# Moving head 1's query blocks behind the first two rows, and head 1's selection to later dots, in a two-block transformer kernel

## What is computed

```python
def second_block(x, ...):
    xn = rms_norm_2(x, ln_mix_g[l])
    proj = xn @ w_in[l]
    a_out = gmlp_spatial_gating(proj[..., :a0], proj[..., a0:a1], gmlp_norm_g[l], gmlp_w_s[l], gmlp_b_s[l])
    b_out = banded_chunk_attention(proj[..., q0:k0], proj[..., k0:v0], proj[..., v0:], ...)
    x = x + jnp.concatenate([a_out, b_out], axis=-1) @ w_out[l]
    x = x + peer_ffn(rms_norm_2(x, ln_ffn_g[l]), peer_w_query[l], peer_sub_keys[l], peer_u[l], peer_v[l])

def block(xb):                                   # peer_ffn, 128 tokens at a time
    q = (xb @ w_query).reshape(PEER_TOKEN_BLOCK, PEER_HEADS, 2, PEER_HALF)
    sc = jnp.einsum('thpd,hpkd->thpk', q, sub_keys)
    s_top, i_top = lax.top_k(sc, PEER_TOPK)
    cand = s_top[:, :, 0, :, None] + s_top[:, :, 1, None, :]
    cand_idx = i_top[:, :, 0, :, None] * PEER_NKEYS + i_top[:, :, 1, None, :]
    best, pos = lax.top_k(cand, PEER_TOPK)       # of the 256 sums
    eidx = jnp.take_along_axis(cand_idx, pos, axis=-1)
    g = jax.nn.softmax(best, axis=-1)
    u = jnp.take(expert_u, eidx, axis=0)
    h = jax.nn.gelu(jnp.einsum('thkd,td->thk', u, xb))
    vv = jnp.take(expert_v, eidx, axis=0)
    return jnp.einsum('thk,thkd->td', g * h, vv)
```

## Time and profile before

| | us |
|---|---|
| median of 3 runs | 1135.32 (1135.18 to 1135.58) |
| the profiled execution | 1135.66 |
| its span, first to last instruction | 1133.9 |
| PE / DVE / ACT / POOL busy | 1044.0 / 756.1 / 571.2 / 374.1 |
| gathers (queue 0) | 272.95 MB, 58.3% of 16 engines' span |

### The profile page before, as it was taken

The page is one execution under the profiler, slowest core; times in us unless marked ns, Lnnn a source line. Parts: engine busy times, 40 slices in busy tenths (PEclk is TensorE's granted clock), DMA queues, the critical chain, the costliest instruction groups (busy, mean ns, idle before and its releaser), DMA issues.

```text
span 1133.9 us, 13438 instructions
## 1 busy us (share of the span) xinstructions
PE 1044.0 (92%) x3994; PEld 653.8 (58%) x3994; DVE 756.1 (67%) x1612; ACT 571.2 (50%) x1327; POOL 374.1 (33%) x285
## 2 busy tenths in 40 slices
PE   9999999999999999999999999998877878787786
PEld 8788888888888887765455555553322322232222
DVE  5765666665545587567777676677668667776755
ACT  7654564544445478445455535444443443444443
POOL 1000000000000000044355545446566666667642
PEclk9999999999999999999999999999999999999999
DMA  9554357865635667789999999999999999999998
GB/s 346 199 162 149 112 181 232 265 212 179 189 105 170 229 216 285 270 323 413 422 419 422 421 420 421 422 421 421 420 422 423 422 421 422 423 421 422 422 422 350
DMA packets 95788, 368.96 MB, mean 325 GB/s; under 512 B 6688, under 2 KB 30264, under 8 KB 63104
## 3 DMA queue, kind: packets, MB, share of 16 engines
q0 software_dynamic: 38368, 272.95, 58.3%
q1 hardware_dynamic: 57376, 95.45, 25.4%
HBM read 367.30 MB, written 1.06 MB: 325 GB/s over the span
## 4 chain that ended last, share of the span: by engine, by line
PE 55%; DMA 21%; ACT 7%; POOL 6%; issue 6%; DVE 4%; POOLq 0%; SPq 0%; ACTq 0%; DVEq 0%
DMA uv_ring<-in_peer_uv,expert 21%; PE gemm L1755 12%; PE gemm L2245 11%; PE gemm L1757 11%; PE gemm L1756 11%; POOL uv_ring L497 6%; PE gemm L2138 3%; PE gemm L2097 2%; DVE uv_ring L1634 2%; PE trb L1749 1%; ACT L946 1%; ACT L924 1%; ACT diag L951 1%; ACT wgt L949 1%; DVE w_both L992 1%
## 5 line engine op out<-in xcount | busy, mean ns | idle before, releaser
L2245 PE MATMUL gemm<-uv_ring,diag 128*128 128x512 f32 x1020 | 486.0, 613 | 83.1 <-ACT diag L951 80.7
L497 POOL DMA_INDIRECT uv_ring<-in_peer_uv,expert x256 | 359.9, 1406 | 320.4 <-PE gemm L2245 178.1
L2245 PEld LDWEIGHTS gemm<-uv_ring,diag 128*128 128x128 f32 x1020 | 182.4, 192 | 357.6 <-ACT diag L951 191.8
L1634 DVE CUSTOM_DVE_ANT_0 uv_ring<-uv_ring,row_of_tile 128x1024 f32<-128x1024 f32 x208 | 254.6, 1224 | 143.9 <-DMA uv_ring<-in_peer_uv,expert 142.4
L992 DVE TENSOR_TENSOR w_both<-raw,w_both 128x1024 fp32r<-128x1024 f32 (+1 forms) x172 | 180.7, 1063 | 130.8 <-ACT w_both L556 130.0
L556 ACT ACTIVATE w_both<-raw 128x1024 fp32r<-128x1024 f32 (+1 forms) x172 | 158.2, 932 | 162.0 <-PE gemm L1757 160.8
L1755 PE MATMUL gemm<-w_both,hT_hi 128*128 128x512 f32 (+1 forms) x512 | 202.7, 396 | 1.0 <-DVE w_both L1058 0.8
L1757 PE MATMUL gemm<-w_both,hT_lo 128*128 128x512 f32 (+1 forms) x512 | 198.0, 387 | 0.0
L1756 PE MATMUL gemm<-w_both,hT_hi 128*128 128x512 f32 (+1 forms) x512 | 197.9, 387 | 0.0
L946 ACT ACTIVATE hid_g<-hid 128x1 f32<-128x1 f32 x208 | 42.2, 203 | 271.1 <-DVE hid L1634 270.7
L1755 PEld LDWEIGHTS gemm<-w_both,hT_hi 128*128 128x128 f32 x512 | 96.2, 188 | 22.8 <-issue 4.0
(11 more groups left out here) (276 smaller groups left out, 836.6 us busy)
## 6 DMA issues: line engine op xcount, KB each, us to landing
raw<-in_w_in SPq DMA_DIRECT2D x30, 1024.0 KB, 5.2
raw<-in_w_gate SPq DMA_DIRECT2D x22, 512.0 KB, 4.0
raw<-in_w_up SPq DMA_DIRECT2D x22, 512.0 KB, 5.0
raw<-in_w_down SPq DMA_DIRECT2D x22, 512.0 KB, 3.2
query<-in_peer_w_query SPq DMA_DIRECT2D x16, 512.0 KB, 9.2
uv_ring<-in_peer_uv,expert POOLq DMA_INDIRECT x259, 12.0
raw<-in_w_ret_o SPq DMA_DIRECT2D x4, 1024.0 KB, 5.2
raw<-in_w_out SPq DMA_DIRECT2D x4, 1024.0 KB, 6.1
```

The lines of the kernel that those rows point to most:

```text
L497: nc.gpsimd.indirect_dma_start(out=uv_ring[k % RING][:, 0:width], out_offset=None, in_=peer_uv, in_offset=bass.IndirectOffsetOnAxis(ap=exp ...
L1634: V.tensor_tensor_reduce(out=u_row, in0=u_row, in1=source, scale=1.0, scalar=0.0, op0=ALU.mult, op1=ALU.add, accum_out=hid[par][:, k:k + 1 ...
L2245: last = nc.tensor.matmul(gemm[b + 2 * n][:], diag[k % RING][:], uv_ring[k % RING][:, D + n * CHUNK:D + (n + 1) * CHUNK], start=(begin and ...
```

## The change

Four things move. No arithmetic changes.

1. **PE, ahead of row 0.** `second_block(0)` leaves its place ahead of `band_values(1)` and now stands behind row 0, `second_block(1)` stays behind row 1. The turned probabilities, one run of 16 transposes behind the last u quarter, become two runs of 8 behind the quarters 1 and 2.
2. **PE, between the rows of heads 0 and 1.** The parts of query block 1 move from behind rows 4, 6, 9, 11 to 6, 9, 12, 14. `scored(1, 0)` moves from row 14 to row 1', `columns_of(0)` from 1' to 2', the `right` quarters from 2', 4', 6', 8' to 3', 5', 7', 9'.
3. **ACT.** The copies of the turned probabilities come ahead of `gmlp_u(1)`, `values_whole(1)` and `mixed_whole(1)` ahead of the exponential of head 0. `taken(1, 0)` moves from row 13 to 15, `scored(1, 0)` from 0' to 3', `whole(0)` from 3' to 4', the square of the right half from 12' to 13'.
4. **DVE.** `gated(1)` moves behind the second eight of head 0, `experts_of` ahead of `soft`. Head 1's pieces stand one dot earlier (7, 7, 8, 8, 8, 9, 9, 10, 10), head 2's one dot later (4' to 12'). The side work behind 11' stays, so it is now ahead of `experts`.

```diff
             first_block_out()
             nc.scalar.preload_act_table(ACT.Gelu_apprx_tanh)
+            probs_columns((2, 3, 4, 5))
             gmlp_u(1)
-            probs_columns((2, 3, 4, 5))
+            values_whole(1)
+            mixed_whole(1)
             nc.scalar.preload_act_table(ACT.Exp)
             scaled("norm4", 1)
             best_exp(0, 0, query_scale(0))
-            values_whole(1)
-            mixed_whole(1)
             nc.scalar.preload_act_table(ACT.Gelu_apprx_tanh)
...
-            weigh(0, 0, scaled_rows=False, after={3: second_blocks_out, 4: second_scores, 7: squared_half(0), 13: taken(1, 0)})
-            weigh(1, 1, scaled_rows=False, after={0: scored(1, 0), 3: whole(0), 12: squared_half(1), 15: whole(1)})
+            weigh(0, 0, scaled_rows=False, after={3: second_blocks_out, 4: second_scores, 7: squared_half(0), 15: taken(1, 0)})
+            weigh(1, 1, scaled_rows=False, after={3: scored(1, 0), 4: whole(0), 13: squared_half(1), 15: whole(1)})
...
                 V.tensor_scalar(neg_best[0][:], best[0][:, 0:1], scales[:, SC_PEER:SC_PEER + 1], -1.0, ALU.mult, ALU.mult).then_inc(best_ready, 1)
+                gated(1)
...
-            gated(1)
             second_eight()
             dots(0, 0, xn[:, 0, :], (0,))
+            experts_of(0, 8, TOPK)
             soft(0, 0)
-            experts_of(0, 8, TOPK)
             late_scores = {0: scored(MM["second_s"]), 1: scored(MM["s_1_0"])}
-            pieces_at = {0: (8, 8, 9, 9, 9, 10, 10, 11, 11), 1: range(3, 12)}
+            pieces_at = {0: (7, 7, 8, 8, 8, 9, 9, 10, 10), 1: range(4, 13)}
             side_work = {0: {5: lambda: out2_row(1, 0)}, 1: {11: lambda: out2_row(1, 1), 15: lambda: variance("norm4", 1)}}
...
-            for q in range(1, 4):
-                u_part(q, 1)
-            turn_band_probs((2, 3, 4, 5))
-            second_block(0)
+            u_part(1, 1)
+            turn_band_probs((2, 3))
+            u_part(2, 1)
+            turn_band_probs((4, 5))
+            u_part(3, 1)
             band_values(1)
             mixed_columns(1)
...
-            add_rows(0, 0, begin=True, after={1: lambda: second_block(1), 2: second_score, 4: part(1, 0, 0), 6: part(1, 1, 0), 9: part(1, 2, 0), 11: part(1, 3, 0), 14: scored(1, 0)})
-            add_rows(0, 1, after={1: columns_of(0), 2: right(2), 4: right(3), 6: right(0), 8: right(1), 13: columns_of(1), 15: part(2, 0, 0)})
+            add_rows(0, 0, begin=True, after={0: lambda: second_block(0), 1: lambda: second_block(1), 2: second_score, 6: part(1, 0, 0), 9: part(1, 1, 0),
+                                              12: part(1, 2, 0), 14: part(1, 3, 0)})
+            add_rows(0, 1, after={1: scored(1, 0), 2: columns_of(0), 3: right(2), 5: right(3), 7: right(0), 9: right(1), 13: columns_of(1), 15: part(2, 0, 0)})
```

## The result

| | before | after |
|---|---|---|
| median, 18 runs each on one chip | 1135.16 (1134.17 to 1137.68) | 1137.32 (1136.86 to 1138.77) |
| profiled execution | 1135.66 | 1137.08 |
| its span | 1133.9 | 1135.3 |

The ratio is 1.0019, 95% interval 1.0013 to 1.0026: the change makes the kernel 2.2 us slower. That is clear of the noise of 18 runs each, since the interval leaves 1 out, though it is just under the 0.2% from which the prediction counted "slower". The forecast was 1138.1, with a range of 1135.2 to 1140.0.

What follows compares the result with a forecast made beforehand. The gathers' DMA flow at 422 GB/s was taken to set the end. Early recoveries of -2.4 us and a new hole of +5.3 at gather 32 gave net +2.8 on 1135.3, so 1138.1, range 1135.2 to 1140.0.

Steps and rivals of the forecast that it cites:

- What bounds the kernel: Gathers at 422 GB/s set the end; a DMA microsecond lost in the transition is one lost at the end.
- Part 1, ahead of row 0: Row 0 comes 2.4 us earlier, at 498.65; the 1.8 us lost at 504 to 511 are recovered.
- Part 2, head 1's experts: Pieces one dot earlier make gather 16 ready near 522 instead of 526.5, recovering 0.6 us.
- Part 3, PE: Row 0 to the end of `right(1)` takes 64.6 us, so `right(1)` ends at 563.2.
- Part 3, DVE and POOL: DVE stalls 2.5 us for `right(1)`; head 2's experts come at 568.1, gather 32 is issued at 569.0, due at 566.3.
- The restart: Gather 32, issued into an empty DMA queue, flows from 571.65 against 568.85 before, 2.8 us later.
- Rival A: Cheap restart: gather 32's bytes follow its issue after 1 to 1.6 us; +1.4, 1136.7; chance 0.11.
- The sum: Over the transition, -2.4 us recovered and +5.3 for the new hole at gather 32: net +2.8 us, median 1138.1.
- B: PE reaches `right(1)` by 560.65, so DVE does not stop: +0.1 to +0.5 us, 1135.6; chance 0.09.
- C: Gather 32 issued by 564.5, the ring never empties and both early holes stay closed: 1132.9; chance 0.09.
- D: Second hole in head 2 or at its end, costing up to 2.5 us: 1138.5 to 1140.6; chance 0.11 with E.
- E: Early part gains nothing: end unchanged, or 2.4 us later, 1140.5, if row 0 stays at 501; chance 0.11 with D.

Runs made afterwards that it cites:

- e1_side_behind_12: Changed kernel with tile 1's side work behind dot 12' instead of 11', so behind head 2's experts: 1135.10, ratio to before 1.0000.
- e2_bunched_experts: Changed kernel with head 2's pieces bunched, its experts behind dot 10' instead of 12': 1133.60, ratio to before 0.9986.
- e5_experts_dot13: Changed kernel with head 2's experts behind dot 13' instead of 12', its other pieces behind 4' to 11': 1138.65, ratio to before 1.0035.
- e7_bunched_side12: Changed kernel with head 2's pieces bunched (experts behind dot 10') and the side work behind dot 12' instead of 11': 1133.61, ratio to before 0.9987.
- e10_bunched_query_back: Changed kernel with head 2's pieces bunched (experts behind dot 10') and `second_block(0)` back ahead of `band_values(1)`: 1134.38, ratio to before 0.9993.
- e6_query_block_back: Changed kernel with only `second_block(0)` put back ahead of `band_values(1)`: 1138.39, ratio to before 1.0031.
- e4_head1_pieces_old: Changed kernel with head 1's pieces back at dots 8, 8, 9, 9, 9, 10, 10, 11, 11: 1137.31, ratio to before 1.0020.

## Why the prediction was right

**What bounds the kernel.** Right. The flow behind 576 is 422 GB/s in both kernels, and the table above is its consequence.

**Part 1, ahead of row 0.** Right in its mechanism, too large in its worth. Row 0 starts at 498.40, forecast 498.65; the dip of 504 to 511 is closed. The later u projection cost nothing that the windows show (369 GB/s from 484 to 504, 362 before). The 1.8 us came from one trace; the two others with the same early program lost 1.0 and 1.2 us there. It could not be paid out in the changed kernel. Where it could, the moved block alone was worth 0.8 (1134.38 against 1133.60). That the turned probabilities bring the 0.5 us put down for them isn't shown: with the block back in its place row 0 starts at 501.09, as before (501.05), because the wait of 0.48 us for ACT is replaced by one of 0.78 for the bank.

**Part 2, head 1's experts.** Right on the trace (gather 16 issued at 522.00, forecast near 522, and 423 GB/s at 527 to 532). As a gain of 0.6 us it isn't borne out: 1133.54 without it, 1133.60 with it.

**Part 3, PE.** `right(1)` ends at 562.6, forecast 563.2. The wait ahead of row 14 has gone: the twelve passes from 535.31 run in one piece, where 1.59 us stood ahead of 536.21. From row 0 to the end of `right(1)` are 64.2 us, forecast 64.6. The 0.3 us that I added for row 0' are the most likely excess; this was not tried.

**Part 3, DVE and POOL.** The stall is 2.46 us, forecast 2.5; side work, dot 12' and experts end at 567.64, forecast 568.1; gather 32 is issued at 568.53, forecast 569.0. All three are earlier by the 0.5 us that PE was. Of this, 0.2 are the whole trace's, since gather 0 goes at 483.68 and not at 483.89. Where only the order of DVE's work was changed (`e1_side_behind_12`, `e2_bunched_experts`, `e5_experts_dot13`), the end moved with the list; where only DVE's stall was (`e7_bunched_side12`), it did not move.

**The restart.** By the lost us, gather 32 counts from 484 + 7.3 + 32 x 2.485 = 570.8, which is 2.3 us behind its issue; I had taken 2.65 of 2.5 to 2.9. This term was too large by 0.3. The rule of the Trainium skill weighed in the prediction (page "DMA: Bandwidth & Descriptors", section "Anatomy of one DMA": about 2.0 us fixed) lies on the other side of it. In the four other traces with a hole of this size (list at 567.9 to 568.7) the same sum gives 2.2 to 2.5, so the measured value lies between the page's and mine. That 1137.5, the sum by the page's figure, is nearer to 1137.32 than mine is partly chance, since PE's chain was shorter too, and since the page puts most of the fixed cost behind the last byte, while the time missing here lies ahead of the first ones. Rival A, a flow 1 to 1.6 us behind the issue, is excluded by the trace: the first bytes are 1.7 us behind it.

**The sum.** The flow at gather 32 is 570.8 - 568.85 = 2.0 us later, forecast 2.8; the missing 0.8 are 0.3 in the restart and 0.5 in PE's chain and the phase. The medians moved by 2.16 and the profiled executions by 1.42; by the slope of the table 2.0 us of flow are 1.7 at the end, with a spread of some 0.6 from one execution to the next, and both lie in that. Taken alone the profiled pair, with less than 2 us, would have met the sign that the prediction gave for rival A; the 18 runs and the first bytes speak against it. The mechanism, its place and the order of the terms were right, and the size was high by a quarter: +2.8 forecast, +2.2 measured. Part of the agreement is luck. The 568.85 come from a trace that had lost 0.6 to 0.7 us more up to 532 than the two others with the same program; with the average of the three it is 568.4. The changed kernel's gather 32 hangs on DVE's list and not on that loss, so against an average trace before my sum would have given some 3.2 us and missed by more. The measured 570.8 - 568.4 = 2.4 us are 2.1 at the end by the slope of the table, as the medians have it. The median lies 0.3 us below the 1137.6 from which I had counted "slower", so by that count the case that came true is "same", with 0.33, and not "slower", with 0.58.

**The rivals.** B (`right(1)` in time) would have needed 560.65 and had 562.6. C, faster than before, was not this kernel, but its mechanism is real: it said gather 32 issued by 564.5 leaves no hole, with 1132.9. With the list made behind dot 10' it was issued at 561.96 and the time was 1133.6. The limit fits: issued at 563.24 (`e10_bunched_query_back`) there was no hole, issued at 565.16 (`e1_side_behind_12`) there was one of 1.2 us. D did not occur: no window behind 576 is low. E did not occur.

## What to carry to other kernels

Where one stream of transfers sets the end, add up what it loses window by window, up to the point from which it never stops; here the difference between two versions of that sum was nearly all of the difference in time, and the engines' busy shares told nothing. Read the sum from more than one trace, since starts differ by some 0.5 us and early dips by more. An early gain in such a stream is worth little until every later list of addresses is early enough to use it, so a list must not stand in a queue behind work that waits for something else: here one edit of a table cost 2.9 us alone and swallowed an early gain of some 2 us. And a wait is costed by what is queued behind it: what was left of the wait for the same matmul, 0.72 us, cost nothing as soon as the list stood ahead of it.

## What the runs showed of the hardware

- A gather queue that has run empty needed 2.2 to 2.5 us from the issue to the time from which its flow counts, in five traces. In steps of 0.2 us the first bytes are 1.7 us behind the issue, at 485.6 before (issue 483.89) and at 570.2 in the changed kernel (issue 568.53). A list 1.1 us ahead of the ring's end (issue 565.16, due 566.3) was not enough and still lost 1.2 us.
- The issue of gather 33 took 1.99 us in the changed kernel, and gather 33 of `e6_query_block_back`, at the same place of the program (570.81), took 0.94. The flow counts from 2.3 and 2.5 us behind gather 32 all the same. What makes an issue on POOL take twice as long was not settled.
- PE waited for ACT for 2.27 us in four kernels: up to 574.63 in the changed one, 572.63 in `e1_side_behind_12`, 575.00 in `e4_head1_pieces_old` and 575.54 in `e6_query_block_back`. In the second the granted clock went to 1.2 GHz at about 572.4 and came back at about 575.8, in the others it stayed at 2.4 GHz. In the second the ring, just refilled, did not cover it: 371 GB/s from 570 to 576. Why the clock fell in one of four is open.
